# Memory keys and values in fp32 from unsplit weights, fill steps moved from the last stretch into single waits, and the attention's ends untied from their neighbours

## The reference

```
mem:  m = rmsnorm(mem, g_mem);  K = m @ w_ck;  V = m @ w_cv           # 256 memory tokens; both are outputs
A/B:  z = rmsnorm(x) @ w_in                                            # 46 slots of 128 columns
      o_ret  = head_norm(retention(rope(q), rope(k), v)) * silu(g)     # 4 heads x 128
      o_rwkv = rwkv7(r, w, k, v, a, g)  with 64-wide lora products     # 8 heads x 64
      x += (gate_a * (o_ret @ w_a) + gate_b * (o_rwkv @ w_b)) @ w_out
attn: x += softmax(q(x) K^T / 16) V @ w_co                             # 4 heads x 256; samples have caches of their own
mlp:  x += relu(rmsnorm(x) @ w_up)^2 @ w_down;  y = rmsnorm(x)
```

## Time and profile before

| | |
|---|---|
| median of 3 runs | 2358.3 us (2356.54 to 2358.79) |
| profiled execution | 2365.18 us, of it 2363.4 us span |
| TensorE clock, mean of the span | 0.984 of full speed |
| PE busy | 2284.2 us, 97% |
| PEld busy | 2178.0 us, 92% |
| DVE busy | 1011.1 us, 43% |
| ACT busy | 437.5 us, 19% |
| POOL busy | 574.1 us, 24% |

### The profile page before, as it was taken

The page is one execution under the profiler, slowest core; times in us unless marked ns, Lnnn a source line. Parts: engine busy times, 40 slices in busy tenths (PEclk is TensorE's granted clock), DMA queues, the critical chain, the costliest instruction groups (busy, mean ns, idle before and its releaser), DMA issues.

```text
span 2363.4 us, 47313 instructions
## 1 busy us (share of the span) xinstructions
PE 2284.2 (97%) x21046; PEld 2178.0 (92%) x21046; DVE 1011.1 (43%) x1276; ACT 437.5 (19%) x759; POOL 574.1 (24%) x292
## 2 busy tenths in 40 slices
PE   6899899999999999999999999999999999999998
PEld 6899888888889899979999987999999999999997
DVE  6633653746536454251535136344314413512423
ACT  5311312314132111142111013111000000000011
POOL 0422201101011022112333210333323323323331
PEclk9999999999999999889999999999999999999999
DMA  6211101102011084226312115111111111111112
GB/s 248 97 45 40 60 10 52 50 25 68 19 53 39 26 243 143 84 77 229 124 45 94 67 49 196 60 45 45 45 45 45 45 45 41 42 46 44 45 45 85
DMA packets 57705, 171.58 MB, mean 73 GB/s; under 512 B 8512, under 2 KB 24256, under 8 KB 54592
## 3 DMA queue, kind: packets, MB, share of 16 engines
q1 hardware_dynamic: 46928, 143.63, 17.5%
q10 hardware_dynamic: 10608, 25.35, 3.0%
HBM read 140.90 MB, written 28.05 MB: 71 GB/s over the span
## 4 chain that ended last, share of the span: by engine, by line
PE 86%; DVE 7%; DMA 3%; ACT 2%; issue 2%; POOL 0%; ACTq 0%; SPq 0%; DVEq 0%; POOLq 0%
PE ps L385 85%; DVE F L1054 2%; DMA z<-zstg 2%; DMA w_raw<-w 1%; DVE TT L1054 1%; DVE w_split L1054 1%; DVE F L1060 1%; ACT F L1641 1%; ACT L1641 0%; DVE T L1054 0%; PE ps L933 0%; DVE F L1057 0%; ACT T L1641 0%; DMA vc<-vc 0%; ACT zstg L1641 0%
## 5 line engine op out<-in xcount | busy, mean ns | idle before, releaser
L385 PE MATMUL ps<-A_s,w_split 128*128 128x364 f32 (+1 forms) x6192 | 1084.4, 333 | 12.0 <-DVE vT L1054 6.0
L385 PEld LDWEIGHTS ps<-A_s,w_split 128*128 128x128 f32 x6192 | 1034.1, 189 | 39.9 <-issue 24.5
L385 PE MATMUL ps<-B_s,w_split 128*128 128x364 f32 (+3 forms) x4032 | 673.5, 329 | 1.4 <-DVE B_s L1054 1.1
L385 PEld LDWEIGHTS ps<-B_s,w_split 128*128 128x128 f32 x4032 | 669.0, 188 | 4.7 <-issue 2.4
L373 POOL CAST w_split<-w_raw 128x1024 fp32r<-128x1024 f32 x140 | 150.8, 1077 | 1690.5 <-PE ps L385 1641.0
L376 POOL TENSOR_TENSOR w_split<-w_raw,w_split 128x1024 fp32r<-128x1024 f32 x140 | 396.2, 2830 | 11.2
L1054 DVE TENSOR_TENSOR F<-ps,F 128x1092 f32<-128x1092 f32 (+3 forms) x52 | 62.8, 1208 | 423.3 <-PE ps L385 423.3
L1641 ACT ACTIVATE B_s<-T 128x1092 fp32r<-128x1092 f32 x32 | 35.8, 1120 | 622.5 <-DVE T L1060 622.5
L1060 DVE SCALAR_TENSOR_TENSOR T<-ps,rsx 128x1092 f32<-128x1092 f32 x32 | 41.5, 1296 | 206.1 <-PE ps L385 198.0
L1054 DVE TENSOR_TENSOR B_s<-T,B_s 128x1092 fp32r<-128x1092 f32 x32 | 105.9, 3309 | 1.1
L1054 DVE TENSOR_TENSOR T<-T 128x1092 f32<-128x1092 f32 x58 | 103.5, 1785 | 1.7 <-DVE w_split L1054 0.2
(11 more groups left out here) (204 smaller groups left out, 2009.4 us busy)
## 6 DMA issues: line engine op xcount, KB each, us to landing
w_raw<-w SPq DMA_DIRECT2D x158, 512.0 KB, 3.5
z<-zstg SPq DMA_DIRECT2D x83, 182.0 KB, 1.9
F<-z SPq DMA_DIRECT2D x16, 546.0 KB, 7.1
kc<-kc SPq DMA_DIRECT2D x7, 1024.0 KB, 4.8
vc<-vc SPq DMA_DIRECT2D x7, 1024.0 KB, 4.9
F<-x SPq DMA_DIRECT2D x8, 546.0 KB, 8.2
Zs<-z SPq DMA_DIRECT2D x16, 273.0 KB, 18.9
Z<-z ACTq DMA_DIRECT2D x8, 546.0 KB, 12.2
```

The source lines that it names most:

```text
L385: return pe.matmul(out, lhsT, rhs, start=start, stop=stop, skip_group_check=skip)
```

## The change

It has three parts.

**A. Memory stage.** The 16 memory slots are no longer split. They are loaded in pairs of slots (1 MB) into one buffer of eight, `raw8`; each key slot is 8 fp32 matmuls of 256 columns (`key_slot`), with the unsplit weights and `memh` as operands. The values are computed with `memh` as the stationary operand and four weight slots as the moving one, 512 columns wide, four tiles of 8 matmuls (`value_tile`): they come out with tokens on partitions, and the transposes, `vT`, `mem_s` and the second weight buffer go. Their factor per token comes from two matmuls of 8 columns. The memory tokens are loaded in two halves with the parameters between them. x is multiplied by its factor on DVE, no longer on POOL; POOL only splits weights, from slot 16 on.

**B. Fill steps.** The fill of 14 steps ahead of the first lora products becomes 22, and the wait for both PSUM sets (`sets_empty`) comes after it. The two fills before bonus sums become 4 steps each (in four pairs, 16 steps more). The fill of 98 in the rotary stage becomes 104. So 30 steps less stand in `fill(cap)`.

**C. Attention.** `scores_of(0)` waits for `g_free[0]` alone; `g_free[1]` is waited for at its fourth head. The first sample's scores stand ahead of `turn(0)`. The last block's values go to another pair of banks and don't wait for the block before. The first unit of `w_co` runs chunk by chunk; its first two chunks (tokens 0 to 727) wait for the first six blocks, the third for all.

```diff
-            pool.wait_ge(rs_ready, 2)
-            for k in range(KT):
-                pool.tensor_tensor(F[:, k, :], F[:, k, :], T0[:, 0, :], ALU.mult).then_inc(hf_ready, 1)
-            pool.wait_ge(w_ready, S_POOL)
-            with pool.Fori(0, (SLOTS - S_POOL) // 2) as i:
+            with pool.Fori(0, (SLOTS - S_PW) // 2) as i:
...
-            def mem_slot(s):
-                open_slot(s)
...
+            def key_slot(s):
+                pe.wait_ge(d_w4[s // 2] if s else d_first, 16)
                 if s >= 6:
+                    pe.wait_ge(g_free[s % 2], (s - 6) // 2 + 2)
                 for k in range(KT):
                     if s == 0 and k % 4 == 0:
                         pe.wait_ge(h_ready, k // 4 + 1)
-                    for n, (wp, xp) in enumerate(((0, 0), (0, 1), (1, 0))):
-                        last = mm(mem_bank(s), w[:, wp, k, :], mem_s[:, k, xp, :],
-                                  start=(k == 0 and n == 0), stop=(k == KT - 1 and n == 2))
+                    last = mm(ps[:, s % 6, 0:MEM], raw8[:, s, k * P:k * P + P], memh[:, k, :], start=(k == 0), stop=(k == KT - 1))
                 last.then_inc(g_done, 1)
...
+            def value_tile(t):
+                g, m = t // 2, t % 2
+                if m == 0:
+                    for i in range(2):
+                        pe.wait_ge(d_w4[2 * g + i], 32)
+                for k in range(KT):
+                    last = mm(ps[:, (0, 3, 1, 4)[t], :], memh[:, k, m * P:m * P + P], raw8[:, 4 * g:4 * g + 4, k * P:k * P + P],
+                              start=(k == 0), stop=(k == KT - 1))
+                last.then_inc(g_done, 2)
...
-            fill(14)
+            fill(22)
+            sets_empty(u)
             pe.wait_ge(lora_act, 2)
...
                     if j:
-                        fill(2)
+                        fill(4)
                     pe.wait_ge(bon_prod, 3 * p + j + 1)
...
-            fill(98)
+            fill(104)
...
-            sets_empty(u)
+            pe.wait_ge(g_free[0], u // 2 + 1)
             pe.wait_ge(d_kvout, 64)
 
             def values(n):
                 pe.wait_ge(at_tc, n + 1)
-                if n:
+                if 0 < n < NA - 1:
                     pe.wait_ge(at_of, 2 * n)
...
                 for h in range(XH):
+                    if n == 0 and h == XH - 1:
+                        pe.wait_ge(g_free[1], u // 2 + 1)
...
             scores_of(0)
             scores_of(1)
+            sample_scores(0).then_inc(as_sc, 1)
...
-            pe.wait_ge(at_of, 2 * NA)
-            pe.wait_ge(as_lo, NSEQ)
-            plain(S_CO, u, 8, B_s)
+            open_slot(S_CO)
+            pe.wait_ge(at_of, 2 * (NA - 2))
+            for c in range(3):
+                if c == 2:
+                    pe.wait_ge(at_of, 2 * NA)
+                    pe.wait_ge(as_lo, NSEQ)
...
+            def x_scaled(k):
+                tt(F[:, k, :], F[:, k, :], T0[:, 0, :], ALU.mult).then_inc(hf_ready, 1)
...
-            load(memx[:, :, :], A["mem"], d_mem)
+            load(memx[:, 0:4, :], A["mem"][:, 0:4, :], d_mem)
             load(par[:, 0:NPAR_IN], A["par"], d_mem)
+            load(memx[:, 4:8, :], A["mem"][:, 4:8, :], d_tab)
...
+            load(raw8[:, 0, :], A["w"][0], d_first)
+            load(raw8[:, 1, :], A["w"][1], d_w4[0])
             sp.wait_ge(d_mem, 32)
-            mem_weights(2)
-            mem_weights(3)
+            weight_pair(1)
             for k in range(4):
                 x_tile(k)
...
+            weight_pair(2)
             for k in range(4, KT):
                 x_tile(k)
+            weight_pair(3)
...
+            for g in range(4, 8):
+                weight_pair(g)
```

More of the change, by code:

```diff
@@ L471, in _ @@
+            for c in range(3):
+                last = mm(ps[:, 5 + c, 0:CH], ones[:, :], T0[:, 1, c * CH:c * CH + CH])
+            last.then_inc(ss_done, 1)
+            pe.wait_ge(g_free[0], 5)
+            pe.wait_ge(g_free[1], 5)
+            for t in range(4):
+                value_tile(t)
+            pe.wait_ge(d_tab, 16 * 6)
             u = 16
             hbase = 2
[L475 to L477 removed]
@@ L1718, in _ @@
-            for k in range(3, KT):
-                if k < 6:
-                    value_out(S_CV + k - 3)
+            a.wait_ge(d_x, 16 * 4)
+            squares(0, 0, F)
+            squares(1, 0, F)
+            a.wait_ge(par_ready, 1)
+            a.wait_ge(ss_done, 1)
+            own.add(act(mrs[:, :], ps[:, 6, 0:MEM], ACT.Ln, scale=1.0 / D, bias=col("rms")))
+            own.add(act(mrt[:, :, :], bank(7, 2, 8), ACT.Ln, scale=1.0 / D, bias=col("rms")))
+            own.wait()
+            act(mrs[:, :], mrs[:, :], ACT.Exp, scale=-0.5).then_inc(rs_ready, 1)
@@ L1721, in _ @@
+            own.add(act(mrt[:, :, :], mrt[:, :, :], ACT.Exp, scale=-0.5))
+            own.wait()
+            for k in range(2, KT):
+                if k == 4:
+                    a.wait_ge(d_xr, 16 * 4)
+                squares(k, 0, F)
+            a.wait_ge(ss_done, 2)
+            root(T0[:, 0, :].rearrange("p (c n) -> p c n", c=3), ps[:, 5:8, 0:CH], 1.0 / D, "rms", rs_ready)
+            for k in range(KT):
                 x_hi(k)
-            for s in range(S_CV + 3, S_PW):
-                value_out(s)
+                if k in (2, 4):
+                    value_out(k // 2 - 1)
```

231 lines of the change are left out of this document (86 added, 145 removed).

## The result

| | before | changed |
|---|---|---|
| median | 2358.55 us (2356.54 to 2362.06, 4 runs) | 2339.95 us (2335.94 to 2344.67, 4 runs) |
| ratio to before | | 0.9923, 95% interval 0.9904 to 0.9942 |
| timed again (e1 below) | 2358.90 us (11 runs) | 2334.98 us (2331.53 to 2337.13, 5 runs) |
| its ratio | | 0.9901, interval 0.9885 to 0.9916 |
| profiled execution, span | 2365.18 us, 2363.4 | 2344.67 us, 2342.9 |

The forecast was 2330, with 8 chances in 10 between 2321 and 2343: the sign and this range held. The narrower range of the forecast's own case, 2325 to 2337, was missed by 3 us at first and held when timed again. The gain came out as 18.6 us, and 23.9 when timed again, where 28.4 were forecast. The changed kernel's profiled execution is the longest of its four.

A forecast was written before the change was run, and what follows sets the result against it. TensorE, busy 97% of the span, bounds the kernel with its work plus 79 us of waiting. Gains 17.5 + 7.0 + 3.9 = 28.4 off 2365.2 give 2336.8, less 6.9 to the median: 2330, 8 in 10 between 2321 and 2343.

The forecast's parts named there:

- the forecast's own case: Whole kernel: all terms hold as summed, 2330 us, own range 2325 to 2337, chance 0.58.
- Part A: Memory stage: the projection's second unit starts at 81.2 instead of 98.69 us, gain 17.5, range 13 to 20.
- The price of fp32: Memory stage: 0.436 us per 256-column fp32 matmul, 27.9 us each for keys and values; four passes would give 62.8.
- The rival on loads: Memory stage bound by its loads, gain of A only 5 to 13 us: 2334 to 2343, chance 0.18.
- The rival on the clock: Memory stage: fp32 matmuls don't wake the clock; at half clock throughout about 2385, chance 0.06.
- the first fill: Ahead of the lora products: PE stands 6.2 us for ACT's copy and loses its clock, loss 3.5, bounds 0 to -5.5.
- the rival without a stall: First fill doesn't stall, part B worth 7 us more: about 2322.6, chance 0.12.
- The bonus sums: Added fills cover waits, gain 6.4 us (5 to 6.4), plus 1.7 (0 to 2) of clock kept with the neighbours.
- The rotary stage: 6 more fill steps, 3.0 us, against a wait of 2.37: gain 2.4 us (1 to 2.4).
- the rival that the moves shift waits: Added fills delay ACT and DVE or side weights come late; B worth nothing or less: 2337 to 2345, chance 0.06.
- Part C: Attention: waits go before the first scores, at the transposes and before w_co, gain 3.9 us, range 2.5 to 4.
- The level: Whole kernel: the median of the runs lies 6.9 us below the profiled execution, taken off the sum 2336.8.

The follow-up runs named there:

- e1: The changed kernel timed and profiled again with no edit: 2334.98 us, ratio 0.9901 to the kernel before.
- e2: Changed kernel with ACT copying the first fill group before its squares, ahead of the wait for xm: 2332.91 us, ratio 0.9887.
- e8: Changed kernel with 2 fill steps instead of 4 ahead of the second and third bonus sum of each pair: 2353.20 us, ratio 0.9979.
- e7: Changed kernel with 98 fill steps in the rotary stage instead of 104: 2332.73 us, ratio 0.9905.
- e12: e9 with SP's loads of raw side weights in the rotary stage ahead of the loads of the retention's values: 2328.17 us, ratio 0.9866.
- e5: Changed kernel with part C undone (attention and first unit of w_co as before): 2341.64 us, ratio 0.9928.
- e6: Changed kernel with the two rounds of the MLP's loop written out on PE: 2333.67 us, ratio 0.9899.
- e11: Changed kernel with one more pair of w_co's units written out, so the MLP's loop starts 144 matmuls later: one execution, 2322.67 us.
- e9: Changed kernel with both ACT's early copy of the first fill group and the MLP's loop written out: 2329.89 us, ratio 0.9861.
- e10: e9 with 16 fill steps of the last stretch moved between the retention's sample products: 2328.47 us, ratio 0.9860.
- e3: Changed kernel with 16 fill steps instead of 22 in the first fill and 12 instead of 6 behind the first lora products: 2332.66 us, ratio 0.9890.
- e4: Kernel before with only the memory stage (part A) changed, fills and attention as before: 2346.91 us, ratio 0.9945.

## Why the forecast gain was 5 to 10 us too large

**Part A, right.** 17.5 against 18.4. The start was 9.0 for 8.3, the cold start cost 8.97 - 16 x 0.437 = 2.0 for 2.65 us. The price of fp32 was the step with the widest claim: 48 key matmuls took 20.97 us, 0.437 each (forecast 0.436), and 32 of 512 columns 27.63, 0.863 (0.872). The Trainium skill's page "FP8 and Floating Point Precision", section "TensorE Precision Notes", has four passes for true fp32; with one column per cycle (the Trainium skill, "TensorE: Matmul & The Clock Gate", section "Step-by-step: what each phase is for") an estimate from the two at 2.4 GHz is 1.67 ns a column. The trace agrees: 27.63 us over 32 x 512 columns are 1.69. What was wrong in the sentence that made 62.8 us of four passes was to multiply the time of a 256-column fp32r matmul, 0.1227 us, which is 0.479 ns a column, where one column per cycle would be an estimate of 0.417. The rival on loads fell: nothing waits in the stage after PE's start. With half a load ahead of the parameters DVE started at 7.63 for 9.27, in the bounds; and PE's first matmul was released by DVE, so that sharing the queues with ACT's load, the Trainium skill's rule in "DMA: Bandwidth & Descriptors", section "Queues, rings and completion order", held up no slot that PE waited for. The rival on the clock fell too: in the window from 14 to 16, with nothing but fp32 keys, it is at its upper level:

```profile
14.00:16.00 2.00, 2.00 (x11) 1.77 (x10) 0.00 (x0) 0.00 (x0) 0.00 (x0) 1.00 1.02 419
```

**Part B, the first fill, right.** Loss 3.5 forecast, 2.8 found; the wait 6.2 forecast, 5.05 found, and the clock fell. So the rival without a stall fell too. e2 shows the cause. It was read from the engine order: the row that waits for `side_out` had passed the lora products.

**The bonus sums, right in one trace and too small on the chip.** 8.1 forecast, 7.4 in the trace, but 18 between the medians of e8 and e1. If the medians are right, the term that was mis-sized is the clock's, "with the neighbours 1.7". It was taken from one execution, and in e8 most executions run at a lower mean clock than the profiled one. That this clock is lost at the bonus sums isn't shown (e8).

**The rotary stage, wrong as a number from one trace.** The forecast set 3.0 us of steps against a wait of 2.37 and said "if ACT's and DVE's times there don't hang on PE". Whether they do isn't settled: the wait at their end was 2.4 to 5.4 us in three traces with the same 98 steps. What was missing besides is that the fill itself can stand, as it did already at 884.59 in the kernel before. Raw weights land 20.5 us after their issue in this stage, a row that was not read:

```profile
Vr<-z SPq DMA_DIRECT2D x4, 546.0 KB, 22.5
w_raw<-w SPq DMA_DIRECT2D x4, 512.0 KB, 20.5
```

and in the first 130 us of the same kernel 4.2 us:

```profile
w_raw<-w SPq DMA_DIRECT2D x23, 512.0 KB, 4.2
```

In the pair of profiles the stage with its six steps lost 0.8 us, in the means of all traces (e7) it gained 1.6. That late weights are the cause was argued from the waits for split weights in the changed kernel. e12, where they landed sooner and the stage was no shorter, doesn't bear it out. So this step failed as a gain read off one execution of a stage whose length varies by 5 to 9 us; the rival that the moves shift waits is borne out by the changed kernel's first trace alone.

**Part C, right in its place, and its gain lost in the MLP.** The attention gained 3.9 us in the profiled pair, as forecast. But the sum had no term for what the written-out unit does to the program behind it: 4.9 us in the mean of six traces at the MLP's jump. This is the larger failed step, an absent one: the forecast counted instructions that run and not where later ones stand. e5 ties the gap to part C, e6 to the jump, e11 to the loop's place. The loads on the instruction queue show what the two kinds of gap differ in (e11); why one place needs one load and another two is open.

**The level.** 6.9 us of distance between profile and median was carried over from the kernel before. Executions of one kernel lie 5 to 23 us apart, so this term can't be trusted to better than about 5 us. Against the span before, the changed kernel's first profile gains 20.5 us and e1's 33.7, the same program. That the median lay in a range 22 us wide is therefore no proof of the sum; the stages are.

The best versions measured are e9, e10 and e12, 2328 to 2330 us, ratios 0.9860 to 0.9866. e11's one execution (2322.67) is shorter still, with the changed kernel's wait in the first fill in it, but its rotary stage (67.7 us) and its half clock around the retention's samples (17 us) are among the shortest of all traces. By the MLP alone the small gap costs 1.0 us against the written-out loop (745.1 and 744.1).

## What to carry to other kernels

When work is moved into a wait, look for what the moved work itself waits for at its new place: here a group's copy that stands late in another engine's order cost 2.8 us and was seen in the order beforehand. Waits inside the rotary stage's own fill stood in the trace before and were not read. Writing a loop's body out can cost as much at the next loop as it gains; read the "issue" waits at each backward jump before and after, with the loads on the instruction queue. Where executions of one kernel differ by 5 us and more, compare the same stretch of several traces, since medians of five or six runs didn't resolve 3 us here.

## What was not expected of the hardware

- The gap at a backward jump of PE goes by the place of the loop in the program: 0.67, 0.79, 0.69 and 0.76 us with the loop at 10183, 9881, 9881 and 10169 rows of matmuls, 3.4 to 4.2 us at 10025 in all six traces. PE went on 2.3 to 2.9 us after the start of a 16 KB instruction load in all ten, the first of the two around the jump in the four with the small gap, the second in the six. Behind the long gap the clock was at half for 3.4 or 6.8 us, a loss of 1.7 to 3.4; behind the small one it didn't fall.
- PE can be busy throughout and stay at half clock for 38 us: from 979 to 1016 in the changed kernel, with eight-column products, fp32 products of half height and fill steps between. With dense products between the eight-column ones the clock held until the half-height ones began (e10).
- The length of a wait alone didn't tell what the clock did. Waits of 3.04 us (e3) and 3.74 (before) ahead of the lora products left it at its upper level, and with the waits of 5.03 to 5.05 us there it fell in all seven traces that have them. But it also fell with 3.84 us there in e4, with 1.63 at 442 in the same trace, with 2.60 and 3.56 in e8, and with 2.23 us in e9, where the same wait in e2 left it up.
